# Second block's opening: two panels side by side, the small products behind them, five filler matmuls

## The chip, the cores and the metric

The kernel runs on one core of one Trainium2 chip. The metric is the device time of one launch in microseconds (us). Three runs of the kernel before gave 1550.59, 1553.88 and 1556.39 us, with a median of 1553.88 us. Every rate and duration below comes from one profiled execution.

## The reference, cut to what matters

The reference is a two-layer first block (a gating and convolution mixer, then attention, each followed by a feed-forward stage), a last RMS norm, and a second block with three mixers and a mixture of 32 experts. The change touches the entry of the second block, where the normed rows are projected:

```python
h = rms_norm_2(x, norm_mix[l]) * (1.0 + scale_m) + shift_m
proj = h @ w_in[l]
m_z, m_xbc, m_dt, sb_qkv, g_qkv, g_a, g_b, g_gate, br_gate = jnp.split(proj, split_points, axis=-1)
```

`h` has 256 rows (tokens) and 1024 features. `m_xbc` (1024 columns) goes through a causal convolution of four taps. `m_dt` (8 columns), `g_a` and `g_b` (4 each) are the 16 columns that the kernel computes as "small products"; decays and step sizes are made from them.

## The kernel before

**Layout.** Activations lie transposed: features on 128 partitions, the 256 tokens along the free axis, 1024 features as eight tiles (KD = 8). A "row tile" i below is one such 128x256 tile of `h`. A weight panel is 128 output features of all 1024 input features, 512 KB, in a ring of four slots.

**A split product.** To keep float32 accuracy at the speed of the rounded type, weights and rows are each split into a high and a low part (w_hi, w_lo, r_hi, r_lo), and `split_matmul` (L688 to L694) issues three matmuls of 256 columns for each panel and row tile: w_hi by r_hi, w_hi by r_lo, w_lo by r_hi. One panel is 8 row tiles by 3, or 24 matmuls, summed in one PSUM bank (`lin[b]`, four of them). ScalarE makes w_hi (L1435) and, in this part of the program, GpSimd makes w_lo (L1842).

**The small products.** For each row tile two float32 matmuls of 16 columns (one for each half of the tokens) multiply `h` itself, as the stationary operand, by 16 columns of `wsmall` (L1032). In the trace each such float32 matmul leaves two records, each with a weight load of 128 columns; the sixteen small products are 32 records.

**What stands around the change.** TensorE runs the last down projection of the first block, then the sums for two norms (L731, L740). ScalarE turns the sums into a scale (L1483 to L1487). VectorE scales row tile i (L2165), ScalarE adds the shift twice, once rounded to r_hi (L1638) and once to `h` (L1639), and VectorE makes r_lo (L2169), which is what the opening waits for through `h_ready`. `keep_warm` (L745) issues filler matmuls of 512 columns into a bank that nobody reads, while TensorE would wait.

**Behind the opening.** When the small products are done (`small_ready`), VectorE takes them (L2175), ScalarE runs four short functions on them (L1645 to L1649), and only then does ScalarE begin with the convolution tiles: L1506 for panel 0, then the split of panel 4 (L1435), and so on, one panel at a time. VectorE does the other taps (L2152). Panels 0 and 1 of the second block are split before the norm, panels 2 and 3 right behind the last shift. Each engine has one queue in program order, so the order of the code is the order of the work. After eight panels TensorE does L1044 (cumulated decays) and 16 more panels.

**The end of the kernel.** The mixture of experts reads its weights from memory with loads that SyncE issues; they wait for buffers that TensorE gives back (L609, L620).

Of the kernel before, what the change touches and what calls it, by code (L numbers as in the profile page):

```python
# [29 lines left out]
P = 128  # L30
T = 256
NT = T // P
D = 1024
KD = D // P
# [148 lines left out]
def program(nc, A, out):  # L183
# [3 lines left out]
    with ctx:  # L187
# [40 lines left out]
        with ExitStack() as first_block:  # L228
# [15 lines left out]
            r_hi, r_lo = sb1("r_hi", [P, KD, T], F32R), sb1("r_lo", [P, KD, T], F32R)  # L244
# [13 lines left out]
        lin = [ctx.enter_context(nc.psum_tensor(f"lin{b}", [P, 512], F32)) for b in range(4)]  # L258
# [7 lines left out]
        panel_done = sem("panel_done")  # L266
# [52 lines left out]
        def ev(name):  # L319

            if name not in events:
                events[name] = sem(name)
            return events[name]
# [340 lines left out]
        def _(pe):  # L664
            seen = Seen()
            panels = Panels(pe)
# [8 lines left out]
            def bank(b, it=None, per=1, later=0):  # L675

                v = panels.free[b] + later
                if it is not None:
                    pe.wait_ge(bank_free[b], it * per + v)
                elif v:  # L680
                    pe.wait_ge(bank_free[b], v)

            def split_panel(j=0, it=None):

                n = panels.n + j
                wait_split(pe, n, it)
                return n % RING

            def split_matmul(o, w, r, start, stop):

                slot, c = w
                pe.matmul(o, w_hi[:, slot, c], r[0], start=start, stop=False, skip_group_check=True)  # L692
                pe.matmul(o, w_hi[:, slot, c], r[1], start=False, stop=False, skip_group_check=True)  # L693
                return pe.matmul(o, w_lo[:, slot, c], r[0], start=False, stop=stop, skip_group_check=True)  # L694
# [19 lines left out]
            def linear(rhs, count, k=KD, first=False):  # L714

                for m in range(count):
                    b = split_panel() if rhs is None else panel()
                    bank(b)
                    if rhs is None:
                        split_linear(b, first and m == 0)  # L720
                    else:
                        product(b, rhs, k, first and m == 0)
                    panels.advance(1)
# [21 lines left out]
            def keep_warm(b, count):  # L745

                pe.wait_ge(bank_free[b], panels.free[b])
                for _ in range(count):
                    pe.matmul(lin[b][:, :], K["ident"], cst[:, 0:512], start=True, stop=True, skip_group_check=True)
# [187 lines left out]
            for j in range(KH):  # L937
                pe.wait_ge(v_normed, j + 1)
                for c in range(NT):
                    mm = pe.transpose(mixbank(c)[:, j * P:(j + 1) * P], v0[:, j, c * P:(c + 1) * P], K["ident"])  # L940
# [5 lines left out]
            for hh in range(8):  # L946
                for c in range(NT):
                    mm = pe.matmul(mixp[64 * (hh % 2):64 * (hh % 2) + 64, hh // 2, c * P:(c + 1) * P],
                                   vt0[:, c, hh * HD:(hh + 1) * HD], wsm0[:, hh, :], start=True, stop=True,
                                   skip_group_check=True)  # L950
# [30 lines left out]
            for g in range(4):  # L981
                if g >= 2:
                    pe.wait_ge(vt1_copied, g - 1)
                for i in range(4):
                    mm = pe.transpose(mixbank(g)[:, i * P:(i + 1) * P],
                                      v1[:, (g % 2) * 4 + i, (g // 2) * P:(g // 2 + 1) * P], K["ident"])
# [3 lines left out]
            for i in range(HEADS + 3):  # L990
# [10 lines left out]
                if 2 <= i <= HEADS + 1:  # L1001
# [4 lines left out]
                    for c in range(3):  # L1006
                        mm = pe.transpose(statbank(g)[:, c * P:(c + 1) * P], p1[:, g % 4, c * P:(c + 1) * P], K["ident"])
# [14 lines left out]
            project((r_hi, r_lo))  # L1022
            keep_warm(panels.n % 4, 4)
            ffn((2,), True)
            keep_warm(2, 3)
            pe.wait_ge(extra_loaded, 80)
            opening = split_panel()
            bank(opening)
            for i in range(KD):
                pe.wait_ge(h_ready, seen(h_ready))  # L1030
                for c in range(NT):
                    mm = pe.matmul(mixbank(0)[:, c * 16:(c + 1) * 16], h[:, i, c * P:(c + 1) * P], wsmall[:, i, 0:16],  # L1032
                                   start=i == 0 and c == 0, stop=i == KD - 1, skip_group_check=True)
                if i == KD - 1:
                    mm.then_inc(ev("small_ready"), 1)
                mm = split_matmul(lin[opening][:, 0:T], (opening, slice(i * P, (i + 1) * P)), (r_hi[:, i, :], r_lo[:, i, :]),
                                  i == 0, i == KD - 1)
            mm.then_inc(panel_done, 1)
            panels.advance(1)
            linear(None, 7)  # L1040
            pe.wait_ge(ev("adt_ready"), 1)
            for c in range(NT):
                for a0, lhs, b0, n in ((0, "upto", 0, 8), (8, "upto64", 8, 4), (12, "ones64", 8, 4), (16, "ones", 0, 8)):
                    mm = pe.matmul(mixbank(1)[:, c * 24 + a0:c * 24 + a0 + n], K[lhs], adt[:, c, b0:b0 + n],  # L1044
                                   start=True, stop=True, skip_group_check=True)
# [53 lines left out]
            for g in range(2):  # L1099
                for c in range(NT):  # L1100
                    mm = pe.matmul(statbank(1)[:, g * T + c * P:g * T + (c + 1) * P], xb[:, 4 + g, c * P:(c + 1) * P],
                                   xb[:, 6 + g, c * P:(c + 1) * P], start=True, stop=True, skip_group_check=True)
# [19 lines left out]
            for at, dst in ((0, mixp), (4, stat)):  # L1122
                pe.wait_ge(sq_ready, seen(sq_ready))
                for i in range(4):
                    mm = pe.matmul(dst[:, i, :], K["ones"], sq[:, at + i, :], start=True, stop=True, skip_group_check=True)
# [1514 lines left out]
```

## Time and profile before

| what | us |
|---|---|
| median of three runs | 1553.88 |
| lowest, highest | 1550.59, 1556.39 |
| the profiled execution's own time | 1550.96 |
| its span in the trace | 1549.2 |
| TensorE busy | 1468.2 |
| mean granted TensorE clock, as a share of full speed | 0.983 |

The span is 1.8 us shorter than the time of the same execution, which lies around it. Times inside the trace count from the span's start. A granted clock of 1.00 is the chip's 2.4 GHz level, 0.50 the 1.2 GHz level; a value between the two is a stretch that holds some of both.

### The profile page before, as it was taken

The page shows a single profiled execution, that of the slowest core. Times are in us where ns is not written, and L with a number is a line of the kernel's source. Part 1 is how long each engine was busy: PE and PEld are TensorE (multiplying, and loading weights), DVE is VectorE, ACT ScalarE, POOL GpSimd, SP SyncE. Part 2 cuts the span into 40 slices and gives each one's busy share as a digit, 9 for nine tenths or more (in the row PEclk, how much of TensorE's full clock was granted, in tenths as well). Part 3 has the DMA queues.
Part 4 walks back from the last instruction along what each step waited for, and adds up shares of the span by engine and source line. Part 5 has one row for each costly group of instructions (what it writes and reads, how often), then busy time and mean ns, then how long its engine had stood idle before and what let it go on. Part 6 is the DMA issues. An engine that isn't in the chain of part 4 may idle for free.

```text
span 1549.2 us, 28384 instructions
## 1 busy us (share of the span) xinstructions
PE 1468.2 (95%) x11254; PEld 1225.1 (79%) x11254; DVE 780.3 (50%) x1409; ACT 573.7 (37%) x929; POOL 294.6 (19%) x121
## 2 busy tenths in 40 slices
PE   7978999999999999999999999999999999989996
PEld 5857999999958999998999898998666666555553
DVE  4954888637674898733453645653322222212122
ACT  2244555445344655436655116444211111111110
POOL 0021222212201121233865001673000000000000
PEclk9989999999999999998999999999999999999998
DMA  8674455574534455652544212477999999999995
GB/s 312 234 275 157 163 164 173 191 255 139 164 137 136 147 174 184 203 175 82 177 137 137 69 55 74 166 256 268 427 424 426 423 425 426 426 427 424 423 426 222
DMA packets 72097, 375.82 MB, mean 243 GB/s; under 512 B 8128, under 2 KB 8384, under 8 KB 49984
## 3 DMA queue, kind: packets, MB, share of 16 engines
q1 hardware_dynamic: 72000, 374.43, 64.1%
q8 instruction: 73, 1.20, 0.3%
q14 instruction: 24, 0.20, 0.0%
HBM read 373.35 MB, written 1.05 MB: 242 GB/s over the span
## 4 chain that ended last, share of the span: by engine, by line
PE 61%; issue 13%; DVE 8%; DMA 8%; SPq 7%; ACT 2%; POOL 1%; POOLq 0%; DVEq 0%; ACTq 0%
PE lin L692 9%; PE lin L693 8%; PE lin L694 8%; DMA moe_low<-in_experts 7%; PE stat L1394 4%; PE mixp L1367 4%; PE mixp L1371 4%; SPq L609 4%; DVE mixers L2034 3%; PE lin L711 2%; PE stat L1327 1%; PE lin L1337 1%; PE stat L692 1%; PE mixp L692 1%; PE stat L693 1%
## 5 line engine op out<-in xcount | busy, mean ns | idle before, releaser
L692 PE MATMUL lin<-r_hi,w_hi 128*128 128x256 f32 x1464 | 426.4, 291 | 11.8 <-POOL w_lo L1838 5.1
L693 PE MATMUL lin<-r_lo,w_hi 128*128 128x256 f32 x1464 | 416.6, 285 | 0.0
L694 PE MATMUL lin<-r_hi,w_lo 128*128 128x256 f32 x1464 | 416.5, 284 | 0.0
L692 PEld LDWEIGHTS lin<-r_hi,w_hi 128*128 128x128 f32 x1464 | 283.4, 194 | 19.8 <-POOL w_lo L1838 6.7
L693 PEld LDWEIGHTS lin<-r_lo,w_hi 128*128 128x128 f32 x1464 | 283.4, 194 | 0.8
L694 PEld LDWEIGHTS lin<-r_hi,w_lo 128*128 128x128 f32 x1464 | 283.2, 193 | 0.0
L1842 POOL TENSOR_TENSOR w_lo<-ring,w_hi 128x1024 fp32r<-128x1024 f32 x71 | 175.4, 2482 | 199.3 <-ACT w_hi L1435 199.2
L1838 POOL TENSOR_TENSOR w_lo<-ring,w_hi 128x1024 fp32r<-128x1024 f32 x42 | 108.3, 2578 | 480.2 <-ACT w_hi L1441 297.9
L1871 DVE TENSOR_TENSOR w_lo<-ring,w_hi 128x1024 fp32r<-128x1024 f32 x126 | 156.5, 1247 | 84.9 <-ACT w_hi L1441 65.1
L1441 ACT ACTIVATE w_hi<-ring 128x1024 fp32r<-128x1024 f32 x124 | 129.6, 1049 | 57.3 <-PE mixp L694 49.0
L1435 ACT ACTIVATE w_hi<-ring 128x1024 fp32r<-128x1024 f32 x119 | 124.1, 1050 | 34.1 <-PE lin L694 16.7
L2546 DVE TENSOR_TENSOR moe_low<-moe_low,mixp 128x256 f32<-128x256 f32 x32 | 13.5, 421 | 207.6 <-ACT moe_low L1812 207.6
L1812 ACT ACTIVATE moe_low<-mixp 128x256 f32<-128x256 f32 x32 | 12.3, 384 | 221.9 <-PE mixp L1371 221.9
L711 PE MATMUL lin<-h,ring 128*128 128x256 f32 x400 | 90.3, 383 | 3.0 <-DVE h L1902 3.0
L711 PEld LDWEIGHTS lin<-h,ring 128*128 128x128 f32 x400 | 75.6, 192 | 16.7 <-issue 6.7
L2553 DVE SCALAR_TENSOR_TENSOR e_y_lo<-stat,moe_high,e_y_hi 128x512 fp32r<-128x512 f32 x32 | 24.0, 751 | 117.3 <-ACT e_y_hi L1817 117.3
L1394 PE MATMUL stat<-moe_high,moe_low 128*64 128x512 f32 x352 | 80.4, 598 | 0.0
L1523 ACT ACTIVATE sgf<-ub 128x256 f32<-128x256 f32 x44 | 18.4, 418 | 119.0 <-DVE ub L1953 119.0
L1367 PE MATMUL mixp<-moe_low,h 128*64 128x256 f32 x352 | 53.3, 381 | 6.1 <-DMA moe_low<-in_experts 3.6
L1367 PE MATMUL mixp<-moe_low,cat 128*64 128x256 f32 x352 | 53.4, 382 | 5.9 <-DMA moe_high<-in_experts 2.9
L1394 PEld LDWEIGHTS stat<-moe_high,moe_low 128*64 128x64 f32 x352 | 23.2, 136 | 40.7 <-issue 37.8
L1817 ACT ACTIVATE e_y_hi<-stat,moe_high 128x512 fp32r<-128x512 f32 x32 | 22.0, 687 | 88.2 <-PE stat L1394 88.2
(485 smaller groups left out, 2795.1 us busy)
## 6 DMA issues: line engine op xcount, KB each, us to landing
ring<-in_panels SPq DMA_DIRECT2D x272, 512.0 KB, 3.8
moe_low<-in_experts SPq DMA_DIRECT2D x64, 1024.0 KB, 22.6
moe_high<-in_experts SPq DMA_DIRECT2D x22, 2048.0 KB, 24.9
aring<-in_ada SPq DMA_DIRECT2D x24, 1024.0 KB, 6.3
ring<-in_experts SPq DMA_DIRECT2D x20, 1024.0 KB, 26.6
moe_high<-in_experts SPq DMA_DIRECT2D x20, 1024.0 KB, 21.9
cst<-in_experts SPq DMA_DIRECT2D x10, 1280.0 KB, 23.5
sq<-in_experts SPq DMA_DIRECT2D x10, 1024.0 KB, 29.5
```

What stands on the lines that cost most here:

```text
L609: sp.dma_start(dst[s][:, 4 * half:4 * half + 4, :].rearrange("p k f -> p (k f)"), A["experts"][e, part, :, half * 2048:(half + 1) * 2048]. ...
L692: pe.matmul(o, w_hi[:, slot, c], r[0], start=start, stop=False, skip_group_check=True)
L693: pe.matmul(o, w_hi[:, slot, c], r[1], start=False, stop=False, skip_group_check=True)
L694: return pe.matmul(o, w_lo[:, slot, c], r[0], start=False, stop=stop, skip_group_check=True)
L711: mm = pe.matmul(lin[b][:, 0:T], w[:, i, :], rhs[:, i, :], start=i == 0, stop=i == k - 1)
L1367: pe.matmul(o[:, 0:T], lhs, gate_weights(slot, k)[:, half * T:(half + 1) * T], start=k == 0, stop=k == KD - 1, skip_group_check=True)
L1394: mm = pe.matmul(statbank(1)[64 * half:64 * half + 64, :], e_hidT[:, k % 2, k // 2, :], down_weights(slot, k, half), start=k == 0, stop=k ...
L1435: act.activation(w_hi[:, n % RING, :], ring[:, n % RING, :], ACT.Copy).then_inc(w_hi_ready, 1)
L1441: act.activation(w_hi[:, n % RING, :], ring[:, n % RING, :], ACT.Copy).then_inc(w_hi_ready, 1)
L1838: pool.tensor_tensor(w_lo[:, POOL_SLOT, :], ring[:, POOL_SLOT, :], w_hi[:, POOL_SLOT, :].bitcast(F32), ALU.subtract).then_inc(w_split_pool, 1)
L1842: pool.tensor_tensor(w_lo[:, n % RING, :], ring[:, n % RING, :], w_hi[:, n % RING, :].bitcast(F32), ALU.subtract).then_inc(w_split_pool, 1)
L1871: dve.tensor_tensor(w_lo[:, n % RING, :], ring[:, n % RING, :], w_hi[:, n % RING, :].bitcast(F32), ALU.subtract)\
```

## The change

Three edits, all in TensorE's program. The fillers behind the first block's last sums become five instead of three. The opening multiplies panels 0 and 1 side by side as each row tile arrives, where it had panel 0 together with the two small matmuls of the tile. The sixteen small matmuls follow as one run behind the last row tile, and `small_ready` is signalled at the end of that run. Six panels follow instead of seven. The number of matmuls of each other kind stays the same.

```diff
             ffn((2,), True)
-            keep_warm(2, 3)
+            keep_warm(2, 5)
             pe.wait_ge(extra_loaded, 80)
-            opening = split_panel()
-            bank(opening)
+            opening = [split_panel(j) for j in range(2)]
+            for b in opening:
+                bank(b)
             for i in range(KD):
                 pe.wait_ge(h_ready, seen(h_ready))
+                for b in opening:
+                    mm = split_matmul(lin[b][:, 0:T], (b, slice(i * P, (i + 1) * P)), (r_hi[:, i, :], r_lo[:, i, :]),
+                                      i == 0, i == KD - 1)
+                    if i == KD - 1:
+                        mm.then_inc(panel_done, 1)
+            panels.advance(2)
+            for i in range(KD):
                 for c in range(NT):
                     mm = pe.matmul(mixbank(0)[:, c * 16:(c + 1) * 16], h[:, i, c * P:(c + 1) * P], wsmall[:, i, 0:16],
                                    start=i == 0 and c == 0, stop=i == KD - 1, skip_group_check=True)
-                if i == KD - 1:
-                    mm.then_inc(ev("small_ready"), 1)
-                mm = split_matmul(lin[opening][:, 0:T], (opening, slice(i * P, (i + 1) * P)), (r_hi[:, i, :], r_lo[:, i, :]),
-                                  i == 0, i == KD - 1)
-            mm.then_inc(panel_done, 1)
-            panels.advance(1)
-            linear(None, 7)
+            mm.then_inc(ev("small_ready"), 1)
+            linear(None, 6)
```

TensorE's row of instructions where the first row tile arrives, before. Here `lin0` to `lin3` are the four banks, `cst` holds the fillers' operands, `wsmall` the sixteen small columns, and an `x2` says that two like instructions stand there:

```order
L740 MATMUL stat<-sq,gains 128x256 x2
L749 MATMUL lin2<-cst 128x512 x3
L1032 MATMUL mixp<-wsmall,h 128x16 x2
L692 MATMUL lin0<-r_hi,w_hi 128x256
L693 MATMUL lin0<-r_lo,w_hi 128x256
L694 MATMUL lin0<-r_hi,w_lo 128x256
L1032 MATMUL mixp<-wsmall,h 128x16 x2
```

The same place with the change:

```order
L740 MATMUL stat<-sq,gains 128x256 x2
L749 MATMUL lin2<-cst 128x512 x5
L692 MATMUL lin0<-r_hi,w_hi 128x256
L693 MATMUL lin0<-r_lo,w_hi 128x256
L694 MATMUL lin0<-r_hi,w_lo 128x256
L692 MATMUL lin1<-r_hi,w_hi 128x256
L693 MATMUL lin1<-r_lo,w_hi 128x256
L694 MATMUL lin1<-r_hi,w_lo 128x256
```

Two fillers are added, and the three matmuls of panel 1 (`lin1`) stand where the two small ones stood.

TensorE's row where the last row tile is done, before:

```order
L1032 MATMUL mixp<-wsmall,h 128x16 x2
L692 MATMUL lin0<-r_hi,w_hi 128x256
L693 MATMUL lin0<-r_lo,w_hi 128x256
L694 MATMUL lin0<-r_hi,w_lo 128x256
L692 MATMUL lin1<-r_hi,w_hi 128x256
```

The same place with the change:

```order
L692 MATMUL lin1<-r_hi,w_hi 128x256
L693 MATMUL lin1<-r_lo,w_hi 128x256
L694 MATMUL lin1<-r_hi,w_lo 128x256
L1040 MATMUL mixp<-wsmall,h 128x16 x16
L692 MATMUL lin2<-r_hi,w_hi 128x256
```

The small matmuls have moved behind the last row tile as a run of sixteen (L1040 is the changed kernel's number for L1032), and panel 2 follows them. The queues of VectorE, ScalarE, GpSimd and SyncE hold the same instructions in the same order as before.

## Rows read from the trace of the kernel before

**Rows 1.** Page, parts 1 and 4: TensorE's share; the chain by engine.
```profile
PE 1468.2 (95%) x11254; PEld 1225.1 (79%) x11254; DVE 780.3 (50%) x1409; ACT 573.7 (37%) x929; POOL 294.6 (19%) x121
...
PE 61%; issue 13%; DVE 8%; DMA 8%; SPq 7%; ACT 2%; POOL 1%; POOLq 0%; DVEq 0%; ACTq 0%
```

**Rows 2.** Stretches: us, length, TensorE busy, granted clock, DMA share, GB/s.
```profile
707.70:709.70 2.00, 0.03 (x1) 1.00 0.00 0
710.60:724.20 13.60, 13.60 (x66) 0.50 0.24 78
724.30:742.80 18.50, 18.50 (x157) 1.00 0.48 152
505.70:506.90 1.20, 0.00 (x0) 1.00 0.00 0
506.90:513.00 6.10, 6.07 (x49) 1.00 0.00 0
1072.80:1075.80 3.00, 3.00 (x30) 1.00 0.54 104
1075.90:1079.20 3.30, 3.30 (x15) 0.50 0.93 390
871.10:874.40 3.30, 3.30 (x12) 0.50 0.00 0
```

**Rows 3.** Chain of work that ended last, 709 to 743 us: start, length, what.
```profile
709.65 0.14 issue
709.79 0.59 PE mixp L1032 x4
...
713.88 0.67 PE mixp L1032 x4
714.55 0.40 PE lin L692
714.95 0.21 PE lin L693
715.16 0.21 PE lin L694
...
726.16 0.12 PE lin L694
...
742.84 1.69 PE mixp L1044 x16
```

**Rows 4.** Timeline, all engines: start, length, engine, line, idle before in brackets.
```profile
704.99 2.74 PE L749 MATMUL lin<-cst 128*128 128x512 f32 x6
...
714.68 1.99 ACT L1435 ACTIVATE w_hi<-ring 128x1024 fp32r<-128x1024 f32 x2
...
714.81 0.43 DVE L2169 TENSOR_TENSOR r_lo<-h,r_hi 128x256 fp32r<-128x256 f32 x1 [0.37 <-ACT h L1639]
...
715.80 4.68 POOL L1842 TENSOR_TENSOR w_lo<-ring,w_hi 128x1024 fp32r<-128x1024 f32 x2 [19.64 <-ACT w_hi L1435]
...
720.56 0.18 DVE L2175 TENSOR_TENSOR arena<-mixp,rows 128x24 f32<-128x24 f32 x1 [5.32 <-PE mixp L1032]
...
723.64 1.05 ACT L1435 ACTIVATE w_hi<-ring 128x1024 fp32r<-128x1024 f32 x1
...
724.08 1.51 DVE L2152 SCALAR_TENSOR_TENSOR arena<-lin,colp,arena 128x255 f32<-128x255 f32 x3
...
724.76 4.84 POOL L1842 TENSOR_TENSOR w_lo<-ring,w_hi 128x1024 fp32r<-128x1024 f32 x2 [4.28 <-ACT w_hi L1435]
```

**Rows 5.** Chain of work that ended last, last 51 us: the experts' final load.
```profile
1498.09 28.67 DMA moe_low<-in_experts
```

**Rows 6.** SyncE's queue, 980 to 1120 us: waited for, us, times, longest.
```profile
SPq L526 <- POOL w_lo L1842: 61.1, 20, 8.3
SPq L609 <- PE mixp L1371: 26.0, 4, 17.6
```

**Rows 7.** Line L2169 over the span: durations min/median/max in ns, first and last start.
```profile
L2169 DVE TENSOR_TENSOR r_lo<-h,r_hi x8: 424/426/428, 709.2 to 714.8; 128x256 fp32r<-128x256 f32 x8
```

## The prediction

> **What bounds the kernel now.** I read the page's first parts first. TensorE is busy 95% of the span and carries 61% of the chain that ended last [rows 1], so an edit to TensorE's program can count one for one. Next come the stretches around the opening, with the granted clock. TensorE stands idle for 2.0 us ahead of it, from 707.7 to 709.7 us. It then works without a gap, but from 710.6 to 724.2 us the granted clock is 0.50, the 1.2 GHz level; behind that it is 1.00 again [rows 2]. So 13.6 us of busy TensorE run at half rate, and that is what can be won here.
>
> The chain shows what one row tile costs in that stretch: 0.67 us for the two small matmuls (four records), then 0.40 + 0.21 + 0.21 = 0.82 us for the three of panel 0, together 1.49 us [rows 3]. That is seven steps of 0.213 us. The row tiles come faster: eight r_lo between 709.2 and 714.8 us [rows 7], one per 5.6 / 7 = 0.80 us. TensorE is the late one, by its clock. At full clock a matmul of a split product takes 0.12 us in the same chain [rows 3], a panel 24 x 0.12 = 2.88 us. My mark for the end of the changed part is the start of L1044 at 742.84 us, behind eight panels [rows 3].
>
> **The change part by part.**
>
> Two more fillers. Three fillers are six records from 704.99 us for 2.74 us; the last record is longer than its pace of about 0.43 us, and ten records end near 704.99 + 2.74 + 4 x 0.43 = 709.45 us [rows 4]. The first row tile lets TensorE start at 709.79 us [rows 3], so they fit with 0.34 us to spare and cost nothing. Were row tiles 0.4 us earlier, they would cost that difference. What they do is fill 1.7 of 2.0 idle us. The nearest precedent is the feed-forward opening at 506.9 us: 1.2 idle us behind four fillers, then two panels side by side, and the clock stays at 1.00 for all of the next 6.1 us [rows 2]. I take it that the changed opening keeps the clock too. The bound from below is the clock of before, which is a rival.
>
> Two panels side by side. At full clock a row tile costs 6 x 0.12 = 0.72 us, less than the 0.80 us in which the next arrives. So the opening ends with the tiles: last r_lo at 714.81 + 0.43 = 715.24 us [rows 4], 0.14 us to react [rows 3], 0.72 us of work: 716.1 us. Both panels were split long before: GpSimd had stood idle 19.64 us when it began with panels 2 and 3 at 715.80 us [rows 4].
>
> The small run. Thirty-two records. No row shows 32 in a row at full clock. The nearest are the sixteen of L1044 in 1.69 us, 0.106 each; the four ahead of the slow stretch take 0.59 us, 0.148 each with a start in it [rows 3]. I take 0.11, near the longer run: 3.5 us, ending at 719.6 us; the bounds are 3.4 and 4.7 us. The records' pace is that of their weight loads, not of 16 columns.
>
> On this the Trainium skill can be read two ways. TensorE: Matmul & The Clock Gate, "Back-to-back issue gap", gives 1 to 64 columns about 25 ns each at full clock; the estimate by that page's table would be 32 x 0.025 = 0.8 us and a gain 2.7 us larger. The 0.106 us of L1044 speaks against it [rows 3], and the same page's section on LDWEIGHTS, 128 columns in about 107 ns, is what the trace agrees with.
>
> Who waits for the small run. Before, VectorE took the small products at 720.56 us [rows 4]; now it can at about 719.8 us, 0.8 us earlier. Behind it in program order stand ScalarE's functions, the convolution's first tile and then the split of panel 4: ScalarE at 723.64 us, GpSimd from 724.76 us for 4.84 / 2 = 2.42 us, to 727.18 us [rows 4]. All of that moves with the small run, to 726.4 us. Panels 2 and 3 have w_lo at 715.80 + 2.34 = 718.1 and 720.5 us [rows 4], ahead of TensorE. TensorE does them from 719.6 to 725.4 us and then waits 1.0 us for panel 4: a new wait that the half clock had hidden. From there GpSimd needs 2.42 us and TensorE 2.88 us a panel, so TensorE sets the pace: L1044 at 726.4 + 4 x 2.88 = 737.9 us. VectorE's 1.51 us a tile [rows 4] frees the banks in time. The SyncE queue is not touched; its loads follow the splits and move with them.
>
> **The sum.** 742.84 - 737.9 = 4.9 us; I write 4.8. With the small run at 4.7 us everything behind it comes 1.2 us later, 3.7 us are won; without the wait for panel 4 it would be 5.9 us. Behind L1044 the chain is TensorE again, and SyncE's expert loads wait for buffers that TensorE gives back, 26.0 us in four waits on L1371 [rows 6], so the whole tail should move along. Against the profiled execution's own 1550.96 us that gives 1546.2 us. That execution is 2.9 us under the median, 1553.88 us, and the result will be a median: 1553.88 - 4.8 = 1549.1 us. A difference of 0.5%, about what a measurement of this kernel can tell from no change, is 7.8 us; the forecast lies within it.
>
> **The rivals.**
>
> A, a short fall of the clock behind the small run. At 1072.8 to 1075.8 us TensorE is busy all 3.0 us with small matmuls of the router, and the following 3.3 us are granted 0.50; there are other such single stretches [rows 2]. The new run is 3.5 us of the same kind. If the fall comes at its end, 3.3 us at half rate cost 1.7 us, of which the wait for panel 4 hides 1.0: gain 4.1 us. If it comes midway, 16 records cost twice 0.106 us, small_ready comes 1.7 us later and so does all behind it: gain 3.1 us. Time 1549.8 to 1550.8 us. The Trainium skill's TensorE page, "Why this matters for your kernels", advises continuous work for throughput; by that advice the small run, which has no gap, would not lower the clock and this rival is void. The trace has a stretch that disagrees.
>
> B, the clock falls as the opening begins, in spite of the fillers, and comes back with the wide matmuls, after some 3.3 us as in the two short stretches [rows 2]. Then 16 matmuls take 0.213 instead of 0.12 us; the opening ends near 717.1 us, 1.0 us late. Gain 3.8 us, 1550.1 us.
>
> C, the other side. The clock stays at half from 710.6 to 724.2 us as now. Then 42 matmuls of the opening at 0.213 us run to 719.5 us, 22 small records to 724.2, ten more at full clock to 725.3 us. small_ready is 4.8 us later than before, w_lo of panel 4 comes at 732.0 us, L1044 at 743.5 us: 0.7 us slower, 1554.6 us. It turns from gain to loss once the small run ends after 724.6 us. Against it: only the mixed opening stayed low so long; stretches of wide matmuls came back sooner [rows 2].
>
> D, the gain is won and given back. The chain's last long piece is a load of 28.67 us [rows 5]; were the expert loads bound to something other than TensorE's progress, the end would stay at 1553.9 us. Against it: the waits in [rows 6].
>
> E, more than the sum. Two later stretches at half clock (871.1 and 1075.9 us [rows 2]) cost 3.3 / 2 = 1.7 us each; if the shift made both go, the gain is 4.8 + 3.4 = 8.2 us, 1545.7 us. Nothing in the change aims at them, and new ones are as likely.
>
> **How the numbers follow.** The forecast has 0.45, A 0.27, B 0.08, C 0.04, D 0.08, E 0.08. The predicted time is 1549.1 us. The cases reach from 1545.7 to 1554.6 us; the three runs of before lie up to 3.3 us from their median, and a new median of a few runs can be off by most of that. So the range is 1543 to 1556 us. Faster by over 0.5% means E, or the forecast with the scatter on its side: 0.12. Slower by over 0.5% has no mechanism of that size here, only C or D with scatter: 0.03. Within 0.5%: 0.85.
>
> **What would show each step right or wrong.** The fillers should end near 709.4 us with under half a us of idle behind them; the granted clock should be 1.00 up to the end of the opening, and the small run should take 3.5 us. ScalarE's first convolution tile should start near 722.4 us, and TensorE should show a wait of about 1 us on GpSimd's w_lo ahead of panel 4. L1044 should start near 737.9 us. A clock of 0.50 within the opening means B or C, behind the small run A. If L1044 comes 5 us earlier and the end does not, D holds. The prediction is wrong as a whole if the clock of before had another cause than the idle time and the small matmuls between the wide ones, since the change removes only these two.

## The result

| | median us | lowest, highest | runs |
|---|---|---|---|
| kernel before | 1550.73 | 1547.64, 1556.39 | 8 |
| changed kernel | 1541.39 | 1537.58, 1545.03 | 8 |

The ratio is 0.9938, with a 95% interval of 0.9922 to 0.9955. The change makes the kernel 9.3 us faster, about 0.6%, where 4.8 us were forecast. The profiled execution of the changed kernel took 1542.16 us, with a span of 1540.3 us. Before it was 1549.2 us.

The page of the changed kernel, parts 1 and 4, answers to [rows 1]:

```profile
PE 1464.2 (95%) x11258; PEld 1219.7 (79%) x11258; DVE 777.9 (51%) x1409; ACT 573.8 (37%) x929; POOL 294.3 (19%) x121
...
PE 63%; issue 13%; SPq 12%; DVE 5%; DMA 5%; ACT 1%; POOL 1%; POOLq 0%; DVEq 0%; ACTq 0%
```

TensorE has four records more (two fillers) and is busy 4.0 us less. That is less than half of the 8.9 us by which the span is shorter, so the rest is idle time that went.

Stretches of the changed kernel, columns as in [rows 2]:

```profile
707.30:707.60 0.30, 0.00 (x0) 1.00 0.00 0
707.60:713.90 6.30, 6.26 (x48) 1.00 0.00 0
713.90:716.90 3.00, 3.00 (x30) 1.00 0.02 5
717.00:723.70 6.70, 6.70 (x33) 0.50 0.48 157
723.80:738.00 14.20, 14.20 (x122) 1.00 0.58 190
867.20:870.50 3.30, 3.30 (x9) 0.50 0.00 0
```

The idle time ahead of the opening is 0.3 us instead of 2.0. The clock stays at 1.00 through the opening (48 records in 6.3 us), but at 717.0 us, near the end of the small run, it falls to 0.50 for 6.7 us. Timeline of the changed kernel (start, length, engine and line), the fillers and the opening, answering to [rows 4]:

```profile
703.70 3.60 PE L749 MATMUL lin<-cst 128*128 128x512 f32 x8
...
707.64 0.36 PE L692 MATMUL lin<-r_hi,w_hi 128*128 128x256 f32 x1 [0.34 <-DVE r_lo L2172]
...
713.97 4.11 PE L1040 MATMUL mixp<-wsmall,h 128*128 128x16 f32 x32
```

The small run took 4.11 us, the last part of it at half clock. The chain of the changed kernel ends the changed part, as the last line of [rows 3] does:

```profile
714.13 3.95 PE mixp L1040 x32
...
738.00 1.69 PE mixp L1047 x16
```

From the first row tile to the cumulated decays (L1044 before, L1047 now) this execution took 738.00 - 707.64 = 30.36 us, where before it was 742.84 - 709.79 = 33.05 us. So 2.7 us of the 8.9 lie in the changed part. A further 2.1 us lie ahead of it: the first row tile came at 707.64 instead of 709.79 us, although no instruction ahead of the fillers differs.

The other 4 us lie behind it, and the largest piece is at the very end. TensorE at the last combine of the experts, before (timeline, the wait by who was waited for, and the DMA traffic from 1538.0 to 1541.1 us):

```profile
1538.32 0.38 PE L1337 MATMUL lin<-e_place,e_y_hi 64*128 64x256 f32 x1 [1.57 <-DVE e_y_lo L2553]
1541.02 0.37 PE L1337 MATMUL lin<-e_place,e_y_hi 64*128 64x256 f32 x1 [2.31 <-issue]
...
1541.61 0.42 PE L1337 MATMUL lin<-e_place,e_y_lo 64*128 64x256 f32 x2
```
```profile
PE lin L1337 <- issue: 2.3, 1, 2.3
```
```profile
q8 instruction: 1, 0.02, 2.9%
```

The same place in the changed kernel:

```profile
1532.77 0.39 PE L1340 MATMUL lin<-e_place,e_y_hi 64*128 64x256 f32 x2 [1.57 <-DVE e_y_lo L2556]
1532.99 0.28 PE L1340 MATMUL lin<-e_place,e_y_lo 64*128 64x256 f32 x2
```

Before, TensorE did one of the sixteen matmuls of the combine and then stood for 2.31 us with no releaser ("issue"); a 0.02 MB packet of instructions, which began at 1538.23 us and took 1.4 us, is the one in the view above. A like packet moves in the changed kernel too (see "The place of the code"), so the packet alone doesn't make the wait. The matmuls behind it took 0.42 us a record pair, at half clock. In the changed kernel the sixteen run through at 0.28 us. From the end of VectorE's last e_y_lo to the start of the last combine matmul it is 4.2 us before and 1.0 us after, so 3.2 us went some 800 us behind the edit.

### The profile page after: what moved, and what is told of

Read it like the earlier page. It is cut to its first block, busy times and chain, and to the rows that moved or that the text cites. A ratio compares the mean times of both kernels' runs of the same rounds, so it can differ in the third digit from the quotient of the medians.

```text
span 1540.3 us, 28392 instructions
## 1 busy us (share of the span) xinstructions
PE 1464.2 (95%) x11258; PEld 1219.7 (79%) x11258; DVE 777.9 (51%) x1409; ACT 573.8 (37%) x929; POOL 294.3 (19%) x121
## 4 chain that ended last, share of the span: by engine, by line
PE 63%; issue 13%; SPq 12%; DVE 5%; DMA 5%; ACT 1%; POOL 1%; POOLq 0%; DVEq 0%; ACTq 0%
PE lin L692 9%; PE lin L693 8%; PE lin L694 8%; SPq L609 5%; PE lin L711 4%; PE stat L1397 4%; PE mixp L1370 4%; PE mixp L1374 4%; DMA moe_low<-in_experts 2%; DMA moe_high<-in_experts 1%; PE stat L1330 1%; PE stat L692 1%; PE mixp L692 1%; PE stat L693 1%; PE stat L694 1%
```

## The experiments

Two numbers say most in what follows. "Opening" is the time from TensorE's first matmul of the first row tile to the first record of L1044 (L1047). "Tail" is the time from the end of the last e_y_lo to the start of the last combine matmul. Each kernel's ratio is to the kernel before on the same chip in the same set of runs.

| kernel | ratio [95%] | opening us | tail us | span us |
|---|---|---|---|---|
| before (same runs as after) | 1 | 32.9 | 4.2 | 1549.2 |
| after | 0.9938 [0.9922, 0.9955] | 30.2 | 1.0 | 1540.3 |
| r1_before_again | 1.0006 [0.9991, 1.0021] | 32.8 | 3.7 | 1550.8 |
| r1_after_again | 0.9944 [0.9923, 0.9966] | 28.3 | 1.0 | 1543.3 |
| r1_fill5_only | 0.9958 [0.9939, 0.9976] | 30.2 | 1.0 | 1542.9 |
| r1_side_fill3 | 0.9996 [0.9979, 1.0013] | 29.6 | 2.9 | 1542.8 |
| r2_before_branch2 | 0.9980 [0.9961, 1.0000] | 32.9 | 1.0 | 1548.3 |
| r2_after_branch62 | 0.9958 [0.9944, 0.9973] | 28.3 | 3.8 | 1541.6 |
| r2_side_mixed | 0.9949 [0.9932, 0.9966] | 27.0 | 1.0 | 1542.2 |
| r2_single_late | 0.9986 [0.9965, 1.0008] | 32.8 | 1.0 | 1548.4 |
| r3_side_fill3_branch2 | 0.9941 [0.9922, 0.9960] | 29.7 | 1.0 | 1545.3 |
| r3_fill5_branch62 | 0.9983 [0.9968, 0.9997] | 30.2 | 4.3 | 1542.3 |
| r3_after_fill871 | 0.9933 [0.9917, 0.9950] | 28.3 | 1.0 | 1537.1 |
| r3_mixed_fill871 | 0.9931 [0.9913, 0.9950] | 27.0 | 1.0 | 1537.6 |
| r4_side3_bad | 0.9991 [0.9975, 1.0007] | 29.7 | 4.4 | 1545.9 |
| r4_side3_good | 0.9959 [0.9945, 0.9973] | 29.7 | 1.0 | 1540.2 |
| r4_side5_good | 0.9936 [0.9920, 0.9953] | 28.3 | 1.0 | 1537.6 |

Openings of kernels with the same code there agree within 0.1 us, the first execution of the change excepted. By the chain, which starts a little earlier or ends a little later, they read up to 0.2 us longer. Spans of single executions differ by several us for the same kernel, since half-clock stretches in the first 150 us of the program come and go: the opening began between 707.6 and 714.6 us, in kernels of each kind.

### The change again, and the kernel before again

Both kernels were taken once more, with nothing edited, to see what repeats.

> The kernel before, unchanged, timed against itself. It gives a second trace of before and the scatter of the comparison. Theory L (only the opening counts; the other parts of the 8.9 us between the two traces are chance): ratio 1.000 within 0.3%, and the second trace differs from the first by some us at the places where the clock falls early (82 to 150 us), in VectorE's L2407 (2.81 us in the first trace of before, 0.61 us in after) and in the 2.3 us that TensorE spends at the last L1337 with no releaser. Theory T (these two belong to the code of before): the second trace has L2407 near 2.8 us and the 2.3 us again.

> The changed kernel, unchanged, for a second trace and a second comparison. Theory L: ratio nearer 0.997 (4 to 5 us) than 0.994, and L2410 (the same instruction as L2407 of before) and the wait at the end differ between its two traces. Theory T: ratio 0.994 again, L2410 short and no wait at the end in the second trace too. In the opening both expect 1.00 of the clock to its end and a fall behind or within the small run, whose place may differ from the first trace.

Stretches of the second execution of the change:

```profile
714.60:720.90 6.30, 6.29 (x48) 1.00 0.00 0
720.90:724.40 3.50, 3.50 (x34) 1.00 0.10 30
724.40:742.80 18.40, 17.56 (x146) 1.00 0.54 183
```

Its waits on row tiles and panels from 700 to 760 us (who waits for whom: us in total, times, longest):

```profile
PE lin L692 <- POOL w_lo L1845: 0.8, 1, 0.8
...
PE lin L692 <- DVE r_lo L2172: 0.3, 1, 0.3
```

Its chain:

```profile
714.61 0.35 PE lin L692
...
721.11 3.49 PE mixp L1040 x32
...
728.83 2.40 POOL w_lo L1845
731.27 0.39 PE lin L692
...
743.04 1.68 PE mixp L1047 x16
```

Here no fall of the clock follows the small run, the run takes 3.49 us, TensorE waits 0.8 us for panel 4's w_lo, and the changed part takes 28.4 us by the chain. The same holds for the three other traces whose code is the same up to there (r2_after_branch62, r3_after_fill871, r4_side5_good): 28.3 us. So the fall at 717.0 us in the first execution came in one of five traces of this code.

The kernel before repeats as well: opening 32.8 us, 13.7 us of half clock, and a wait of 1.8 us at the last combine. Set beside it, the change in the same set of runs accounts for its span like this: first row tile 0.7 us later, opening 4.6 us shorter, the way from L1044 to the experts' first gather 1.7 us shorter (340.4 to 338.7), from there to the last e_y_lo 1.0 us longer, tail 2.7 us shorter, the rest 0.1 us shorter. That sums to 7.4 of the 7.5 us between the spans.

### Each part of the change alone

The fillers alone, on the kernel before:

```diff
-            keep_warm(2, 3)
+            keep_warm(2, 5)
```

> Before with five fillers instead of three, nothing else. If the idle 2.0 us alone drops the clock, the mixed opening now runs at 1.00, a row tile takes the 0.80 us of its arrival and L1044 comes 5 us or more earlier than 33.0 us behind the first row tile: ratio about 0.997. If the small matmuls between the wide ones drop it, the clock falls within the opening all the same, L1044 stays at 32 to 33 us behind the first row tile and the ratio is 1.000. Theory T by code size: the end is as in after, without the 2.3 us wait, since TensorE's program has grown by the same two matmuls; theory T by time: it stays if the opening does not gain.

The order alone, with three fillers, on the changed kernel:

```diff
-            keep_warm(2, 5)
+            keep_warm(2, 3)
```

> The changed kernel with three fillers as before. If the fillers matter, the clock falls in the opening after the 2.0 us of idle and L1047 comes about 1 us later than the 30.4 us behind the first row tile of after (the rival B of the prediction), ratio 0.995 to 0.997. If only the small matmuls between the wide ones dropped the clock, it is like after. Theory T by code size: the 2.3 us wait at the end is back, as TensorE's program is as long as before.

Five fillers alone: the clock holds through the mixed opening and falls later, for 3.4 us, and the opening takes 30.2 us.

```profile
711.50:717.90 6.40, 6.39 (x55) 1.00 0.00 0
718.00:730.10 12.10, 10.29 (x86) 1.00 0.53 173
730.20:733.60 3.40, 3.40 (x18) 0.50 0.01 6
```

So the small matmuls between the wide ones don't make the long stretch by themselves: with these still there and only 1.7 us of idle filled, the 13.7 us of half clock are gone. The idle time doesn't make it by itself either. The order alone, with all 2.0 us of idle left, gives 29.6 us: the clock falls as the opening begins, but for two stretches of 3.4 us instead of one of 13.7. The long stretch is seen only where both are there. Each part alone wins 2.7 to 3.2 us of the opening, both together 4.6.

The times did not follow the openings. Five fillers alone measured 0.9958, 6.5 us faster, though they win 2.7 us locally; the order alone measured 0.9996, no change, though it wins 3.2. The two traces differ at the tail: r1_fill5_only has no wait there, and r1_side_fill3 has one of 1.7 us. r1_side_fill3 has no more instructions than the kernel before, and r1_fill5_only has two more matmuls. That made the place of the code the suspect.

### The place of the code

The combine stands in the other branch of an If that this input takes. In the trace a record of the instruction queue carries 0.02 MB. My theory: TensorE's program comes in blocks, and one block's edge lies behind the first combine matmul, so that TensorE has to wait there for the next block. The two fillers move all code behind them on by eight instructions, and with it the edge's place among the combine's matmuls. The Trainium skill bears on this in "Runtime: NRT & Kernel Launch", section "Instruction fetch mechanics": the program comes in 16 KiB blocks of 256 instructions, a crossing is mostly hidden, and a branch breaks the sequential prefetch. The 0.02 MB packet agrees with the block's size; "mostly hidden" holds in the changed kernel and not in the one before, where the wait is 2.3 us.

The packet itself is in every trace. The changed kernel from 1532.7 to 1533.9 us, where TensorE works through the combine without a wait:

```profile
q8 instruction: 1, 0.02, 5.4%
```

In all seventeen traces one such packet starts 2.8 to 3.3 us ahead of the end of the last e_y_lo, and another between 0.2 us ahead of that end and 0.4 us behind it. So the fetch doesn't start because TensorE stands. What differs is what TensorE does meanwhile: in the eleven traces without the wait it works on, and in the six with it the next matmul starts 1.2 to 1.5 us behind the end of the second packet (before: packet 1538.23 to 1539.64 us, matmul at 1541.02 us). That fits a block whose instructions are wanted at once in the one case and not in the other. Whose instructions the packets hold, no trace shows.

To move the edge and nothing else, matmuls were put into the branch that this input never takes, so the executed work is unchanged. Each such float32 matmul leaves two records and two weight loads, four instructions, so the change's two fillers add eight (11258 matmul records and as many weight loads, where before has 11254 of each):

```diff
             with pe.If(more == 1):
+                for _ in range(2):
+                    pe.matmul(mixbank(0), K["ident"], third_u[0], start=True, stop=True, skip_group_check=True)
```

That is r2_before_branch2, on the kernel before. r2_after_branch62 has `range(62)` in the same place on the changed kernel: 248 instructions, which with the change's eight are 256. If that is one whole block, the edge comes back to where it was.

> Before, with two more 512-column matmuls in the branch of TensorE's program that the input never takes (for experts with more than 64 tokens), which stands ahead of the last combine. Nothing more is executed; only the place in memory of the last combine's code moves, by the same two matmuls that the fillers add. Theory T by code place: the wait at the last L1337, 2.3 and 1.8 us in the two traces of before, is gone and the kernel is 2 to 3.5 us faster, ratio about 0.998, with the clock in the opening as before. Theory L: no change, ratio 1.000, wait still there.

> The changed kernel, with 62 such matmuls (248 instructions, a block of code of 16 KB less the 8 that the two fillers add) in the branch that is never taken. The last combine's code then lies in its block where it lay in before. Theory T by code place: the wait at the last combine is back, 2 to 3 us, and the ratio is 0.996 to 0.997 instead of 0.994. Theory L: like the changed kernel.

The tail of r2_before_branch2, with the wait gone:

```profile
1540.77 0.38 PE L1337 MATMUL lin<-e_place,e_y_hi 64*128 64x256 f32 x2 [1.58 <-DVE e_y_lo L2555]
1540.99 0.28 PE L1337 MATMUL lin<-e_place,e_y_lo 64*128 64x256 f32 x2
```

The tail of r2_after_branch62, with the wait back:

```profile
1531.12 0.38 PE L1340 MATMUL lin<-e_place,e_y_hi 64*128 64x256 f32 x1 [1.57 <-DVE e_y_lo L2558]
1533.40 0.37 PE L1340 MATMUL lin<-e_place,e_y_hi 64*128 64x256 f32 x1 [1.90 <-issue]
```

The opening of r2_before_branch2 is as slow as before, 32.9 us with 13.6 us at half clock, and yet the tail is 1.0 us:

```profile
709.00:711.00 2.00, 0.00 (x0) 1.00 0.00 0
712.40:726.00 13.60, 13.60 (x66) 0.50 0.24 78
```

Its span is only 0.9 us shorter than that of before, and this execution has 10.2 us at half clock from 1081.1 us on, where all others but r2_single_late have pieces of 3.4 us. From L1044 to the last e_y_lo it took 796.8 us, against 793.6 in r1_before_again.

This settles that the wait goes with the code's place and not with the opening. By time the place is worth 0.2%, 3 us, on the kernel before, with an interval that just reaches 1.0000. On the changed one it is 0.9958 against 0.9936 to 0.9944 in other sets of runs, 2 to 3 us, with intervals that overlap. The tails in the traces of these kernels differ by 2.7 to 3.2 us. The pair of runs on one chip further down has intervals that don't overlap.

The same was then done crosswise: the order with three fillers and the good place, and five fillers alone with the bad one (the edits are those above, `range(2)` and `range(62)`).

> The changed opening with three fillers, and two matmuls in the branch that is never taken, so that the last combine's code lies as in the changed kernel. It differs from the changed kernel in the two fillers' execution alone. If the fillers act through the clock alone: the wait at the last combine is gone (3 us), and the ratio is the 0.9996 of three fillers less 0.002, so 0.997 to 0.998; the second trace of this opening shows whether the first one's 29.6 us from the first row tile to L1047 was lucky: with the clock of before it would be 31 to 33 us. If the fillers act through the code's place alone, it is like the changed kernel, 0.994.

> Before with five fillers, and 62 matmuls in the branch never taken, so that the last combine's code lies as in before. What is left is what the fillers do in the opening. Two causes add up: ratio 0.9958 plus 0.002, so 0.9975 to 0.998 (3 to 4 us faster than before), L1044 30 us behind the first row tile and the wait at the end back. If the code's place were all, 1.000.

The tail did what the theory says both times (1.0 and 4.3 us). Five fillers at the bad place measured 0.9983 instead of 0.9958, so by these ratios 3.9 of that kernel's 6.5 us were the place; what is left, 2.6 us, is about what it wins in the opening, 2.7 us. The two intervals overlap, so the times alone don't show this split. The order with three fillers measured 0.9941 where I had expected 0.997 to 0.998, a step of 0.55% from 0.9996, more than the traces show. These two numbers came from one chip but from two sets of runs, so the pair was run again in one set, with the change beside it.

> The changed kernel with three fillers, code of the last combine as in before. If the parts add up (the traces give 3.2 us for the opening): ratio 0.997 to 0.998. If 0.9996 was right, 1.000, and something outside the traced opening gives the gain back.

> The same with two matmuls in the branch that is never taken. If the code's place is worth what the traces show at the last combine, 3 us or 0.2% below r4_side3_bad: 0.995 to 0.996. If 0.9941 was right, 0.994 and the place is worth more than the traces show.

> The changed kernel once more beside them. If the two fillers' execution is worth the 1.4 us by which its opening is shorter in three traces of four (28.3 against 29.7 us), 0.1% below r4_side3_good; if they act through the code's place alone, equal to it.

In one set of runs the place is worth 0.9991 to 0.9959, 5 us, against 3.4 us in the tails of the traces. The two intervals don't overlap, and each reaches 2.2 to 2.5 us to either side, so 3.4 us lie within the scatter. The two fillers executed ahead of the opening are worth 0.9959 to 0.9936, 3.6 us, with intervals that overlap. Stretches of r4_side3_good show what they are for:

```profile
709.50:710.60 1.10, 1.10 (x9) 1.00 0.00 0
710.70:714.10 3.40, 3.40 (x18) 0.50 0.00 0
714.10:721.00 6.90, 6.90 (x62) 0.99 0.25 78
721.10:724.40 3.30, 3.30 (x18) 0.50 0.44 159
```

With 2.0 us of idle left, the clock falls 1 us into the opening, and once more behind the small run. That costs 1.4 us of the opening (29.7 against 28.3). A further 1.6 us lie at 871 us, below, and it isn't shown that the fillers win them.

### Other openings

r2_side_mixed keeps five fillers and two panels side by side, but does each row tile's small matmuls in the tile's turn, as before, and signals `small_ready` there. This separates "no idle, two panels" from "small products as one run".

```diff
             for i in range(KD):
                 pe.wait_ge(h_ready, seen(h_ready))
+                for c in range(NT):
+                    mm = pe.matmul(mixbank(0)[:, c * 16:(c + 1) * 16], h[:, i, c * P:(c + 1) * P], wsmall[:, i, 0:16],
+                                   start=i == 0 and c == 0, stop=i == KD - 1, skip_group_check=True)
+                if i == KD - 1:
+                    mm.then_inc(ev("small_ready"), 1)
                 for b in opening:
```

> Five fillers, panels 0 and 1 side by side, but the two small matmuls of each row tile ahead of them as in before. At full clock a row tile costs 4 x 0.11 + 6 x 0.12 = 1.16 us, the opening 9.3 us and small_ready comes at its end, 0.3 us ahead of where after has it. If the small run is what drops the clock behind the opening, this kernel has no fall there and L1044 comes 28 us behind the first row tile, ratio 0.994 or below. If mixing is what drops it, the clock falls within the opening, 29 to 31 us, ratio 0.995 to 0.997.

r2_single_late keeps five fillers and the small run behind, but only one panel in the opening:

```diff
-            opening = [split_panel(j) for j in range(2)]
+            opening = [split_panel(j) for j in range(1)]
...
-            panels.advance(2)
+            panels.advance(1)
...
-            linear(None, 6)
+            linear(None, 7)
```

> Five fillers, only panel 0 as the row tiles arrive, the sixteen small products as one run behind it, then seven panels. TensorE works 0.36 of each 0.80 us in the opening. If the second panel beside the first is worth its 2.88 us, L1044 comes 2.5 to 3 us later than in after (31 us behind the first row tile, more if the thin opening drops the clock), ratio 0.996 to 0.998. If the gain is the fillers' alone, it is like the kernel with five fillers only, 0.996.

The mixed opening with two panels has the shortest opening of all:

```profile
714.30:723.00 8.70, 8.70 (x75) 1.00 0.01 2
723.00:741.30 18.30, 18.16 (x150) 1.00 0.59 191
```

TensorE is busy from the first tile to the mark but for 0.14 us, the clock stays at 1.00, and `small_ready` comes at 8.7 us behind the first tile instead of 10.0; the opening takes 27.0 us. So the run behind the opening costs 1.3 us against the mixed order, once the clock holds. By time the two can't be told apart (0.9949 and 0.9944).

With one panel nothing is won:

```profile
711.10:719.30 8.20, 7.02 (x45) 1.00 0.00 0
719.40:726.20 6.80, 6.80 (x33) 0.50 0.47 157
726.30:743.80 17.50, 17.50 (x148) 1.00 0.47 154
```

TensorE waits 1.2 us for row tiles, the clock falls in the small run for 6.8 us, and the opening takes 32.8 us. The second panel would use the time between row tiles. It is 4.5 us behind the change's 28.3. How much of that is the panel's 2.88 us of work, done later, and how much the half clock, this run doesn't tell.

### The half-clock stretch at 871 us

In the traces without the change a stretch of 3.4 us at half clock stands behind a wait of 2.2 us on VectorE at L1170 [rows 2]; it was absent in three of the four traces with the changed opening, and in r3_fill5_branch62, though the wait is there in all of them. The kernel before:

```profile
871.03 1.97 PE L1170 MATMUL stat<-cst,arena 128*128 128x128 f32 x8 [2.22 <-DVE arena L2319]
```

The change, second execution:

```profile
871.24 1.10 PE L1173 MATMUL stat<-cst,arena 128*128 128x128 f32 x8 [2.22 <-DVE arena L2322]
```

To see what the stretch is worth, two fillers were put ahead of that wait, on the change and on the mixed opening:

```diff
+            keep_warm(panels.n % 4, 2)
             pe.wait_ge(ev("g_mt_ready"), 1)
```

> The changed kernel with two more fillers in TensorE's 2.2 idle us ahead of L1173 (863 to 873 us), behind which five of eight traces so far have the clock at 0.50 for 3.4 us. If the idle time is what drops it there, this stretch goes and the kernel is 0 to 1.7 us faster than the changed one, ratio 0.993 to 0.994. If two fillers of 1.7 us are not enough or come at the wrong place, equal to it.

> Five fillers, panels 0 and 1 side by side with the small matmuls of each row tile ahead of them, and the two fillers ahead of L1173. Small_ready comes with the end of the opening and there is no run of small matmuls by itself: L1044 27 us behind the first row tile as in the first kernel with this order. If both stretches at half clock are gone, this is the fastest, ratio 0.993; if the clock falls in the mixed opening in some runs, it is no better than the changed kernel.

The same place in r3_mixed_fill871:

```profile
864.41 1.88 PE L749 MATMUL lin<-cst 128*128 128x512 f32 x4
866.79 1.10 PE L1174 MATMUL stat<-cst,arena 128*128 128x128 f32 x8 [0.50 <-DVE arena L2323]
```

The idle is 0.5 us, and the stretch is in neither trace. From L1044 to the first gather the mixed opening took 340.25 us without these fillers and 338.67 with them; the traces of the change without the stretch took 338.4 to 338.7, the one with it 340.8. So the stretch is worth 1.6 to 2.4 us. By time neither kernel can be told from the change (0.9933 and 0.9931 against 0.9936 to 0.9944): no version here beats the change by more than its scatter.

## Why the prediction was wrong

The forecast for the changed part was right, and the time was wrong, because more than that part moved. Point by point, by its steps:

- **The fillers.** Right. They end at 707.30 us and the first row tile starts TensorE at 707.64 us, 0.34 us spare as said.
- **The opening at full clock, with the tiles.** Right: in r1_after_again the 48 records take 6.3 us, as forecast.
- **The small run.** Right at 3.49 us, where 3.5 were taken. The 25 ns for each by the Trainium skill's table ("TensorE: Matmul & The Clock Gate", "Back-to-back issue gap") would have made 0.8 us; the trace disagrees with that reading.
- **The new wait for panel 4.** Right: 0.8 us, said 1.0.
- **The changed part.** 28.4 us against 28.1 by its own numbers, a gain of 4.6 us where 4.8 were forecast, in four of five traces.
- **Rival A.** It came true in the first profiled execution: the clock fell at 717.0 us for 6.7 us, where 3.3 were taken, and the gain in that part was 2.7 us, less than the 3.1 it allowed. One of five executions is close to the chance of 0.27. In all four traces of the new order with three fillers, and in the one with a single panel, half clock also came in the small run or within 0.7 us behind it. The Trainium skill's advice in "Why this matters for your kernels" (same page), by which gapless work keeps the clock, holds in four traces and not in that one.
- **Rivals B and C.** Neither occurs with the five fillers. B is what three fillers with the new order show (r4_side3_good).
- **Rival D.** Nothing was given back.
- **Rival E.** In the three traces of the change where the clock held in the opening (without the fillers at 871 us), both stretches are gone. The one at 871 us is worth 1.6 to 2.4 us. The one behind the router was mis-priced at 1.7 us: it is worth nothing, since from the router's last small product to the experts' first gather it is 9.9 to 10.1 us with it (before, r1_before_again, the first execution of the change) and 9.9 to 10.0 us without it (those three traces), with TensorE waiting for VectorE in between. The chance of 0.08 was too low. That the change makes them go is not shown: the stretch behind the router is missing in r1_fill5_only and r1_side_fill3 too, and the wait ahead of 871 us is the same 2.22 us with the stretch and without. Rows of the router's place in r1_after_again:

```profile
1068.00:1071.60 3.60, 3.60 (x35) 1.00 0.31 60
1071.60:1075.00 3.40, 3.40 (x23) 1.00 0.90 354
```

**The step that failed** is "so the whole tail should move along". It took everything behind L1044 as fixed in length. It is not: the tail holds a wait of TensorE of 1.7 to 2.5 us that depends on where the code lies, and adding two fillers moves the code. The wait of 2.3 us with no releaser stood in the waits of the kernel before, and the sum put it at nothing without a reason. The account of the 9.3 us by the traces without rival A is then 4.6 for the opening, 2.7 to 3.2 for the tail, and 1.6 to 2.4 for the stretch at 871 us: 8.9 to 10.2 us. The last term is not shown to belong to the change.

A second term was mis-sized, the time it all starts from. The median was taken at 1553.88 us from three runs; eight put it at 1550.73. Of the 7.7 us between the predicted 1549.1 and the measured 1541.39 us, 3.1 are this and 4.5 the gain. The result lies 1.6 us below the range's lower end of 1543 us, so with either term right the range, moved along with it, would have held the result. With a better median alone it would have hidden the step that failed.

**What stays open.** The order with three fillers at the bad place measured only 0.6 and 1.4 us faster than before (0.9996 and 0.9991), though its traces show 3.2 us less in the opening. The intervals reach to 0.9979 and 0.9975, 3.3 and 3.9 us, so scatter may make the difference. The traces are also each of one execution: that of r1_side_fill3 took 1544.56 us, 3.5 us under its kernel's median, that of r3_fill5_branch62 4.6 us under, and that of r3_side_fill3_branch2 4.2 us above. Something in unprofiled executions may differ from the traces, and no run here shows it.

## What to carry to other kernels

Read the waits with no releaser over the whole span before costing a local edit: where the code lies decides some of them, and here eight more instructions some 800 us ahead were enough to move one of them. To know what an edit is worth in itself, time it also with padding in a branch that isn't taken, so that the code behind it stays where it was. Idle time ahead of a dense stretch can cost more than its own length: here 1.7 us of idle cost about 2.7 us of the old opening, and 1.4 us of the new one. Fillers that ended 0.34 us ahead of the first row tile's matmul cost nothing.

## What was unexpected of the hardware

**The place of the code.** Where the combine's code lies behind the branch decides a wait of 1.7 to 2.5 us; that a block's edge in it is the reason is argued from the 256 instructions and the packets. In five of six traces the matmuls behind it run at half clock. From e_y_lo to the last combine matmul it is 2.9 to 4.4 us in the six traces with the wait, and 1.0 in all eleven without.

**The clock.** The same code can keep it or lose it. Filling 1.7 of 2.0 us of idle ended the long half-clock stretch in both traces with the old order, while the small run of the change lost the clock in one of five.

**VectorE and GpSimd together.** In the profiled execution of before, a product of VectorE took 2.88 us, where 0.69 is usual. VectorE and GpSimd, kernel before:

```profile
972.40 2.88 DVE L2407 TENSOR_TENSOR arena<-arena,cst 128x512 f32<-128x512 f32 x1
```
```profile
972.38 5.12 POOL L1842 TENSOR_TENSOR w_lo<-ring,w_hi 128x1024 fp32r<-128x1024 f32 x2 [0.77 <-ACT w_hi L1435]
```

The same two in r1_before_again (one timeline, GpSimd's first product by itself):

```profile
976.49 2.92 POOL L1842 TENSOR_TENSOR w_lo<-ring,w_hi 128x1024 fp32r<-128x1024 f32 x1 [0.78 <-ACT w_hi L1435]
976.50 0.69 DVE L2407 TENSOR_TENSOR arena<-arena,cst 128x512 f32<-128x512 f32 x1
```

In all seventeen traces GpSimd's product starts 0.01 to 0.02 us ahead of VectorE's, and one of the two is longer than usual each time. In before it is VectorE's, 2.2 us longer, while GpSimd's took 2.35 us. In the sixteen others it is GpSimd's, 2.92 to 2.94 us instead of the 2.36 to 2.43 us of the products just ahead and behind, while VectorE's took 0.69. So the overlap is there each time, and which engine pays is what varies. In before it is 2.2 us of the way from L1044 to the experts (342.6 us against 340.4). The Trainium skill, "GPSIMD Engine Reference", section "Specifications", says that GpSimd shares its memory interfaces with VectorE and contends with instructions of two inputs; that fits, and what decides which of the two waits, no experiment here was made on.
